# Second block of a two-block transformer kernel: rotations in their own PSUM bank and one tile behind the head sums; output projection started on three head pairs before the last

## The reference

```python
proj = h @ w_in[layer]
(qa, ka, va, qb, kb, vb, qi, ki, wi, qc, kc, vc) = jnp.split(proj, split_points, axis=-1)
qa = apply_partial_rope(rmsnorm(heads(qa, N_HEADS_A), qk_g[layer, 0]), cos, sin)   # and ka, qb, kb
qi = apply_partial_rope(qi.reshape(B, S, IDX_HEADS, IDX_DIM), cos, sin)            # and ki, without a norm
oa = moba_attention(qa, ka, heads(va, N_HEADS_A))       # 4 heads
ob = dsa_attention(qb, kb, heads(vb, N_HEADS_B), qi, ki, wi)   # 4 heads, keys picked by an indexer
oc = stick_breaking_attention(heads(qc, N_HEADS_C), heads(kc, N_HEADS_C), heads(vc, N_HEADS_C))  # 8 heads
o = jnp.concatenate([oa, ob, oc], axis=2)
o = _rms(o) * out_g[layer]        # per head of 64
x = x + g2 * (o @ w_out[layer])
```

## Time and profile before

| | us |
|---|---|
| median of 3 runs (lowest, highest) | 3065.47 (3065.07, 3066.64) |
| the profiled execution, its own time | 3064.59 |
| its span | 3062.4 |
| PE busy in the span | 2942.2 (96%) |
| DVE busy | 2088.6 (68%) |
| ACT busy | 1314.9 (43%) |
| POOL busy | 205.2 (7%) |

### The profile page before, as it was taken

How to read it: one execution, slowest core, us unless ns; L and a number is a source line. 1 busy time by engine, 2 the same in 40 slices (tenths; PEclk the granted TensorE clock), 3 DMA queues, 4 the chain that set the end, 5 groups by cost and what they waited for, 6 DMA issues and landing times.

```text
span 3062.4 us, 52325 instructions
## 1 busy us (share of the span) xinstructions
PE 2942.2 (96%) x23184; PEld 2868.1 (94%) x23192; DVE 2088.6 (68%) x2644; ACT 1314.9 (43%) x1300; POOL 205.2 (7%) x163
## 2 busy tenths in 40 slices
PE   8999999999999999999999999999799999997999
PEld 8999998999999999999999999988599999885999
DVE  7777867556776668857657767767667766776554
ACT  5344545444333345544444343344543433445332
POOL 0000420000000001500000000011000000110000
PEclk9999999999999999999999989999899999998999
DMA  7654433435666644433446646633056566431354
GB/s 271 241 201 174 143 124 136 167 138 207 238 216 237 244 179 166 138 127 135 167 159 223 256 168 234 249 136 138 14 215 243 203 250 241 170 112 40 138 180 150
DMA packets 78464, 549.07 MB, mean 179 GB/s; under 512 B 8480, under 2 KB 11936, under 8 KB 12320
## 3 DMA queue, kind: packets, MB, share of 16 engines
q1 hardware_dynamic: 67152, 464.99, 42.4%
q0 software_dynamic: 11088, 80.75, 6.5%
HBM read 544.65 MB, written 1.05 MB: 178 GB/s over the span
## 4 chain that ended last, share of the span: by engine, by line
PE 80%; DVE 12%; ACT 4%; issue 2%; POOL 2%; DMA 0%; DVEq 0%; POOLq 0%; SPq 0%; ACTq 0%
PE ps L301 72%; DVE ring_lo L295 3%; ACT w_hi L288 2%; PE ps L373 1%; PE ps L747 1%; PE ps L497 1%; POOL qk L1492 1%; DVE hk L1201 1%; POOL rope_a L1488 1%; PE ps L877 0%; DVE e L400 0%; DVE e L1259 0%; DVE e L1258 0%; DVE a_hg L1279 0%; PE ps L1610 0%
## 5 line engine op out<-in xcount | busy, mean ns | idle before, releaser
L295 DVE TENSOR_TENSOR ring_lo<-ring,w_hi 128x2048 fp32r<-128x2048 f32 x438 | 1009.0, 2306 | 646.4 <-ACT w_hi L288 641.7
L301 PE MATMUL ps<-h_hi,w_hi 128*128 128x256 f32 x4688 | 1350.9, 288 | 39.9 <-DVE h_lo L2004 17.2
L301 PE MATMUL ps<-h_lo,w_hi 128*128 128x256 f32 x4688 | 1336.0, 285 | 0.0
L301 PE MATMUL ps<-h_hi,ring_lo 128*128 128x256 f32 x4688 | 1335.0, 285 | 0.0
L288 ACT ACTIVATE w_hi<-ring 128x2048 fp32r<-128x2048 f32 x438 | 837.1, 1911 | 727.6 <-PE ps L301 663.1
L301 PEld LDWEIGHTS ps<-h_hi,w_hi 128*128 128x128 f32 x4688 | 909.8, 194 | 52.0 <-issue 44.8
L301 PEld LDWEIGHTS ps<-h_lo,w_hi 128*128 128x128 f32 x4688 | 909.9, 194 | 4.6 <-issue 4.0
L301 PEld LDWEIGHTS ps<-h_hi,ring_lo 128*128 128x128 f32 x4688 | 909.5, 194 | 0.0
L301 PE MATMUL ps<-g_hi,w_hi 128*128 128x256 f32 x1408 | 398.5, 283 | 0.0
L301 PE MATMUL ps<-g_lo,w_hi 128*128 128x256 f32 x1408 | 398.5, 283 | 0.0
L301 PE MATMUL ps<-g_hi,ring_lo 128*128 128x256 f32 x1408 | 398.5, 283 | 0.0
(11 more groups left out here) (307 smaller groups left out, 3130.0 us busy)
## 6 DMA issues: line engine op xcount, KB each, us to landing
ring<-stream SPq DMA_DIRECT2D x438, 1024.0 KB, 4.8
e<-ada POOLq DMA_DIRECT2D x77, 1024.0 KB, 5.1
x<-x_t SPq DMA_DIRECT2D x4, 256.0 KB, 4.9
mem<-mem_t SPq DMA_DIRECT2D x1, 1024.0 KB, 10.3
out_t<-x SPq DMA_DIRECT2D x4, 256.0 KB, 2.1
con_sb<-con SPq DMA_DIRECT2D x1, 896.0 KB, 14.9
con_sb<-con SPq DMA_DIRECT2D x1, 640.0 KB, 5.9
hq<-lmask SPq DMA_DIRECT2D x1, 512.0 KB, 15.6
```

Of the source, the lines that this page charges most:

```text
L295: nc.vector.tensor_tensor(ring_lo[:, p % RING, :], ring[:, p % RING, :], w_hi[:, p % HIGHS, :].bitcast(F32), ALU.subtract).then_inc(S.w_lo ...
L301: mm = nc.tensor.matmul(out, a, b, start=start and n == 0, stop=stop and n == 2, skip_group_check=group)
```

## The change

In each layer of the second block:

- `rotate` writes bank 4 in place of bank 3. `head_sums(j)` no longer waits for `rot_scaled` of group j-1 but for `head_var` of group j-1 (the DVE read of bank 3), and the first one for `mod_ready`, a wait that stood ahead of `rotate(0)`.
- PE: `tile(4)` comes before `head_sums(3)`; then `tile(j+1)`, `head_sums(j)`, `rotate(j-1)` for j = 4 to 6; then `tile(8)`, `rotate(6)`, and a wait for the last `rot_scaled` before the logits, whose first unit uses bank 4 too. The logits thus stand behind tile 8.
- ACT: `evac(4)` before `head_rstd(3)`, and so on; `evac(8)` before the logits.
- DVE: `rope` is cut into `head_var`, `head_norm` and `turn`; for j = 4 to 6 the order is `head_var(j)`, `turn(j-1)`, `low` of tile j+4, `head_norm(j)`. One more `low` stands ahead of the scoring, and those in and behind it move on by one.
- The output projection's tiles 0 and 1 are summed over the blocks of pairs 0 to 2 as these come ready, onto a bank filled with zeros; then both get the blocks of pair 3. Tiles 2 and 3 are as they were.

```diff
...
             def head_sums(j):
 
                 pe.wait_ge(S.head_sq, nth(S.head_sq, j - NORMED + 1))
-                pe.wait_ge(S.rot_scaled, nth(S.rot_scaled, j))
+                if j > NORMED:
+                    pe.wait_ge(S.head_var, nth(S.head_var, j - NORMED))
+                else:
+                    pe.wait_ge(S.mod_ready, nth(S.mod_ready, 2))
                 nc.tensor.matmul(ps[:, 3, :], C(C_BD, P),
                                  e_buf[1][:, 2 * (j - NORMED):2 * (j - NORMED) + 2, :].rearrange("p k t -> p (k t)"),
                                  start=True, stop=True).then_inc(S.head_ss, 1)
...
                     pe.wait_ge(S.head_ready, nth(S.head_ready, j - NORMED + 1))
                 else:
                     pe.wait_ge(S.evac_done, nth(S.evac_done, j + 1))
-                    if j >= 1:
-                        pe.wait_ge(S.rot_scaled, nth(S.rot_scaled, j))
+                if j >= 1:
+                    pe.wait_ge(S.rot_scaled, nth(S.rot_scaled, j))
                 r = HD if n == 1 else P
-                nc.tensor.matmul(ps[0:r, 3, 0:n * T], con_sb[0:r, C_R2:C_R2 + r],
+                nc.tensor.matmul(ps[0:r, 4, 0:n * T], con_sb[0:r, C_R2:C_R2 + r],
                                  fq[0:r, at:at + n, :].rearrange("p k t -> p (k t)"),
                                  start=True, stop=True).then_inc(S.rot_done, 1)
 
             tile(0)
             tile(1)
-            pe.wait_ge(S.mod_ready, nth(S.mod_ready, 2))
             rotate(0)
             tile(2)
             rotate(1)
...
                 mm = nc.tensor.transpose(ps[:, 2, T + t * P:T + (t + 1) * P], fq[:, 4, t * P:(t + 1) * P], ident)
             mm.then_inc(S.wi_ready, 1)
             rotate(2)
-            for j in range(NORMED, N_ROPE):
+            tile(4)
+            head_sums(3)
+            for j in range(NORMED + 1, N_ROPE):
+                tile(j + 1)
                 head_sums(j)
-                tile(j + 1)
-                rotate(j)
+                rotate(j - 1)
+            tile(8)
+            rotate(6)
+            pe.wait_ge(S.rot_scaled, nth(S.rot_scaled, N_ROPE))
...
-            for n in range(8, 15):
+            for n in range(9, 15):
                 tile(n)
 
             def scores(n):
...
                     weigh(n, st[:, 6 + n % 2, :], (HEADS_2 + n) * HD, T, S.a_ready, S.o_done)
             pe.wait_ge(S.arg_ready, nth(S.arg_ready, HEADS_2))
             pe.wait_ge(S.scores_read, nth(S.scores_read, HEADS_2))
-            pe.wait_ge(S.o_ready, nth(S.o_ready, HEADS_2 // 2))
-            for b in range(4):
+
+            def out_part(b, n, j):
+
+                for k in (j, 4 + j):
+                    mm = triple(ps[:, b, n * T:(n + 1) * T], weights(Z_O + b, k * T + n * P, k * T + (n + 1) * P),
+                                both(h2, k), False, True, True)
+                return mm
+
+            for b in range(2):
+                nc.tensor.matmul(ps[:, b, :], zeros[:, 0:P], zeros[:], start=True, stop=True)
+                pe.wait_ge(S.w_lo_ready, Z_O + b + 1)
+                for n in range(2):
+                    for j in range(3):
+                        pe.wait_ge(S.o_ready, nth(S.o_ready, j + 1))
+                        out_part(b, n, j)
+            pe.wait_ge(S.o_ready, nth(S.o_ready, 4))
+            for b in range(2):
+                for n in range(2):
+                    mm = out_part(b, n, 3)
+                mm.then_inc(S.tile_done, 1)
+            for b in range(2, 4):
                 project(pe, Z_O + b, b, h2)
...
             nc.scalar.activation(w_idx[:].rearrange("p (t n) -> p t n", t=2),
                                  ps[:, 2, T:2 * T].rearrange("p (t n) -> p t n", t=2)[:, :, HD:HD + IDX],
                                  ACT.Copy).then_inc(S.wi_ready, 1)
+            evac(4)
+            head_rstd(3)
+            evac(5)
             act.wait_ge(S.rope_done, nth(S.rope_done, 3))
             nc.scalar.activation(fq[HD:P, 4, :], fq[0:HD, 4, :], ACT.Copy).then_inc(S.ki_ready, 1)
-            for j in range(NORMED, N_ROPE):
-                head_rstd(j)
-                evac(j + 1)
+            head_rstd(4)
+            evac(6)
+            head_rstd(5)
+            evac(7)
+            head_rstd(6)
+            evac(8)
             act.wait_ge(S.head_ready, nth(S.head_ready, N_ROPE - NORMED))
...
-            for n in range(8, 15):
+            for n in range(9, 15):
                 evac(n)
 
             def exps(n):
...
             gain(chain, 2)
             chain(nc.vector.tensor_scalar(parts[8], parts[8], 0.5, None, ALU.mult))
 
-            def rope(j):
+            def head_var(j):
+                i = j - NORMED
+                vv = e_buf[0][:, 2 * i:2 * i + 2, :].rearrange("p k t -> p (k t)")
+                dve.wait_ge(S.head_ss, nth(S.head_ss, i + 1))
+                nc.vector.tensor_scalar(vv, ps[:, 3, :], 1.0 / HD, EPS, ALU.mult, ALU.add).then_inc(S.head_var, 1)
+
+            def head_norm(j):
+                i, (at, n) = j - NORMED, ropes[j]
+                vv, rr = (e[:, 2 * i:2 * i + 2, :].rearrange("p k t -> p (k t)") for e in e_buf)
+                dve.wait_ge(S.head_rs, nth(S.head_rs, i + 1))
+                refine(chain, rr, vv)
+                dve.wait_ge(S.evac_done, nth(S.evac_done, j + 1))
+                part = fq[:, at:at + 2, :].rearrange("p k t -> p (k t)")
+                g = V2_QK + (2, 3, 0, 1)[i]
+                nc.vector.scalar_tensor_tensor(out=part, in0=part, scalar=v_now[:, g:g + 1], in1=rr,
+                                               op0=ALU.mult, op1=ALU.mult).then_inc(S.head_ready, 1)
+
+            def turn(j):
                 at, n = ropes[j]
                 r = HD if n == 1 else P
...
                 dve.wait_ge(S.rot_done, nth(S.rot_done, j + 1))
                 if j >= 1:
                     dve.wait_ge(S.rope_done, nth(S.rope_done, j))
-                nc.vector.tensor_tensor(rope_b[0:r, 0:n, :], ps[0:r, 3, 0:n * T].rearrange("p (a t) -> p a t", a=n),
+                nc.vector.tensor_tensor(rope_b[0:r, 0:n, :], ps[0:r, 4, 0:n * T].rearrange("p (a t) -> p a t", a=n),
                                         con_sb[0:r, C_SIN:C_SIN + T].unsqueeze(1).broadcast_to([r, n, T]),
                                         ALU.mult).then_inc(S.rot_scaled, 1)
 
             low(dve, Z_QI + HIGHS)
-            for j in range(N_ROPE):
-                if j < NORMED:
-                    low(dve, Z_QI + j + 1 + HIGHS)
-                rope(j)
-                if j >= NORMED:
-                    low(dve, Z_QI + j + 1 + HIGHS)
+            low(dve, Z_QI + 1 + HIGHS)
+            turn(0)
+            low(dve, Z_QI + 2 + HIGHS)
+            turn(1)
+            turn(2)
+            low(dve, Z_QI + 3 + HIGHS)
+            head_var(3)
+            low(dve, Z_QI + 4 + HIGHS)
+            head_norm(3)
+            for j in range(NORMED + 1, N_ROPE):
+                head_var(j)
+                turn(j - 1)
+                low(dve, Z_QI + j + 1 + HIGHS)
+                head_norm(j)
+            turn(6)
+            low(dve, Z_QI + 8 + HIGHS)
 
...
                 if r % 3 == 2:
-                    low(dve, Z_V + 1 + r // 3 + HIGHS)
+                    low(dve, Z_V + 2 + r // 3 + HIGHS)
...
-            for n in range(3, 8):
+            for n in range(4, 8):
                 low(dve, Z_V + n + HIGHS)
 
             def soften(n):
```

13 lines of the change are left out of this document (removed).

## The result

| | us |
|---|---|
| before, median of 3 (lowest, highest) | 3065.47 (3065.07, 3066.64) |
| changed, median of 3 (lowest, highest) | 3026.30 (3025.48, 3029.37) |
| ratio | 0.9875, 95% interval 0.9862 to 0.9889 |
| profiled execution of the changed kernel | 3025.48, span 3023.4, granted clock 0.98 |
| forecast | 3025 (3016 to 3037) |

A forecast was written before the change was run, and what follows sets the result against it. A chain was taken as the bound: PE's head sums waiting for the sine product (15.1 us), its output projection for the last low part (17.2). 12.1 + 8.2 = 20.3 us a layer, 40.6 for both, gave 3025 us, range 3016 to 3037.

The forecast's parts named there:

- Rotations, 12.1 us a layer: Rotation 0 to attention: 13.6 us less at full clock, 1.5 charged for one slow stretch; bounds 10.6 and 13.6.
- the walk: Step-by-step timing of layer 0's new order from row durations: tiles 7.2 us apart, logits from 2091.0, attention from 2130.7.
- The 1.5 us charged for a slow stretch: Behind the loop's last waits: 14 matmuls at the lower clock, 0.22 us each for 0.12.
- Waits: PE in the rotation loop: rotations wait 1.5, 0.2, 0.8 and 0.6 us for the norm, the logits 1.4.
- the rival that the turn's bank frees little: Rotation loop: only the 4.93 us wait and its 1.5 us slow stretch go, 3036 us in all; chance 0.08.
- Output, 8.2 us a layer: Output projection: pairs 0 to 2 summed ahead save 8.9 us at full clock, 7.6 with 14 slow matmuls; middle taken.
- the full-clock case (8.9): Output projection: 8.9 us less a layer if no matmul of it runs at the lower clock.
- The rival of sums at the lower clock throughout: Output projection: 60 matmuls 0.10 us slower each, gain only 2.9 us a layer, 3035.5 us in all; chance 0.08.
- POOL holds low parts: Rotation loop: POOL's sum holds two of DVE's low parts a layer by 0.8 us each; 2 us in all, 3027; chance 0.20.
- DVE in time behind the loop: Behind the loop: tile 14's low part ends at 2120.9, tile starts 2124.9, 4 us cover; rival DVE bound, 3032, chance 0.15.
- The stream doesn't starve: Rival in the tile stream: PE outruns DMA landings of 19 us or more; at 20 us 3073 us; chance 0.03.
- the sign I gave for being wrong: Output projection: the forecast is wrong if the residual behind the last tile waits for a low part.

The follow-up runs named there:

- small sum: The changed kernel with POOL's sum of the rotated group cut to 1 of 256 columns of each half: 3023.03 us (ratio 0.9864).
- before, filled: The kernel before, with matmuls of zeros into an unused bank in PE's waits of the rotation loop: 3061.38 us (ratio 0.9986).
- output packed: The changed kernel with sums over pairs 0 and 1 in PE's waits at the attention's end, tile 2 also summed ahead: 3022.79 us (ratio 0.9865).

## Why the prediction was right, point by point

- **What bounded the kernel**: right. The two waits named there are gone, and PE does the same matmuls.
- **Rotations, 12.1 us a layer**: 11.9 was measured in both. That it is so close is luck, since three errors in it cancelled. (1) The norms come 1.1 us late from norm 4 on, since POOL's sum holds a refining step. I had taken refine and gain at 2.93 us from a row with no sum beside it, and had written that the sums hide because the next turn comes 5 us later; they hide from the turn, not from the norm. In the walk tile 6 ends at 2073.9 and norm 5 at 2082.2, 8.3 later; measured are 2074.2 and 2083.4, 9.2 later. The logits so begin at 2093.4 and not 2091.0, though rotation 0 came 0.5 us sooner; of these 2.9 us the sum accounts for 2.1 (small sum). (2) The logits took 3.86 us and not 5.1, 1.2 less: the row I took them from the earlier trace rows was itself in part at the lower clock. (3) The 1.5 us charged for a slow stretch didn't occur; the stage is at 1.00. The attention starts at 2131.9, for 2132.2 with the charge.
- **Waits**: 0.67, 0.31, 0.34 and 1.18 at the rotations and 0.78 at the logits, for 1.5, 0.2, 0.8, 0.6 and 1.4. Right in kind: rotations wait for the norm, the logits for the last sine product.
- **The bank**: the rival that the turn's bank frees little put the gain at 6.4 us a layer, waits and clock. In the changed kernel it is 11.9, so that rival is out. The bank alone is worth 4.0 by the stages of one fast execution and 1.9 by the medians; the lag gives the rest.
- **Output, 8.2 us a layer**: 8.3 and 9.2. Measured from the last pair the norm comes 15.75 us behind, against 15.8 in the walk; that is the full-clock case (8.9), but in layer 0 the attention ahead of it took 0.7 us longer up to the last sum of squares (59.07 for 58.38). So the middle between full and lower clock, which I had taken, was right for a reason that I hadn't given. The rival of sums at the lower clock throughout is out.
- **POOL holds low parts**: the exclusion held and the place was wrong. In the loop of the changed kernel ACT's high part was ready when DVE came to the low part, once by 0.03 us, so there is no gap of 0.5 us ahead of it for the sum to slip into. The sum comes second, and what it holds is the next operation, the refining step, which I had left out. It costs 2.1 us a layer (small sum), more than the rival's 1. The case that I had described, sum first and low part held, does occur in before, filled, where the gap is 0.27 us and the hold 1.0.
- **DVE in time behind the loop**: right. The low part for tile 14 ends at 2122.9, tile 14 begins at about 2126.1; 3.2 us of cover where 4 were forecast. The stream doesn't starve: a tile of it still lands 4.8 us after its issue, and PE's waits for a low part are 2.4 us in the whole program, as before.
- **Residual behind the last tile**: the sign I gave for being wrong is there in small: the last residual at 2216.46 starts directly behind a low part, some 0.1 us after it could. It costs next to nothing yet; in output packed it is the bound.
- **The missing 1.4 us** of the total: the edited stages lost 41.2 us, more than the 40.6 forecast, and the rest of the program took 2.2 more. It was 0.5 us less ahead of rotation 0, 2.3 more in the feed-forwards and 0.4 more at the end. All together the rest wasn't longer at the lower clock (81.9 us for 82.5); only the feed-forwards and the end were, by 6.8 and 2.9 us, and 10.2 us less of it ahead of rotation 0 made that stretch only 0.5 us shorter.

What stays open is why the clock in stretches with a full PE and unchanged code is now lower, now not, and what else moves them: the stretch ahead of rotation 0 took from 2038.9 to 2045.6 us over these kernels. Its time at the lower clock explains that in part only. With 64.9 us of it the kernel before took 2040.4, and with 61.4 output packed took 2042.3. Nothing here was made to settle that.

## What to carry to other kernels

When a dependent pair of matmuls shares a bank and a slot between two tiles, give the second its own bank and let it lag a tile; the bank alone moved the wait to the next producer, and only the lag hid it. Before forecasting from durations, look whether the row was taken at full clock and with no GpSimd operation beside it: a chain of low part, sum and next step was worth 2.1 us a layer. When an order is changed, look at what now stands behind each operation beside which GpSimd works: the same sum cost nothing while a reading of PSUM stood there. Judge an edit of a few us by the length of the stages it touches, since untouched ones moved the total by up to 8.6 us.
